# Mixture-of-experts layer on one Trainium2 core: expert outputs scaled when they leave PSUM and added to their tokens by accumulating scatters, bias and residual summed on TensorE in the last stage, one expert tile a turn

## The reference, cut to what matters

```python
x = layer_norm(DN_ALPHA * x + g1 * mix, ln1_g, ln1_b)      # kept in DRAM as x1
h = modulate(x, sh2, sc2)                                   # kept in DRAM as h2
logits = t @ w_router + b_router
top_vals, top_idx = top_k(logits, 4)
probs = softmax(top_vals)
# rows sorted by expert; for each (token, choice) of an expert:
gu = xs @ w_gu[e] + b_gu[e]
act = (min(up) + 1) * min(gate) * sigmoid(1.702 * gate)     # with clips at 7
out = act @ w_down[e] + b_down[e]
ffn[token] = sum over its 4 choices of probs * out
x = layer_norm(DN_ALPHA * x + g2 * ffn, ln2_g, ln2_b)
```

## Time and profile before

| | |
|---|---|
| time, median of 3 runs | 6377.13 us (6376.93 to 6379.13) |
| the profiled execution's own time | 6380.74 us |
| its span in the profile | 6379.1 us |
| mean granted TensorE clock | 0.96 of full speed (2.4 GHz) |
| PE, PEld, DVE, ACT, POOL busy | 93%, 75%, 71%, 49%, 15% of the span |
| `combine`, from its first instruction to the end | 6137.4 to 6379.1 us |

### The profile page before, as it was taken

How to read it: one execution, slowest core, us unless ns; L and a number is a source line. 1 busy time by engine, 2 the same in 40 slices (tenths; PEclk the granted TensorE clock), 3 DMA queues, 4 the chain that set the end, 5 groups by cost and what they waited for, 6 DMA issues and landing times. The chain is left out here.

```text
span 6379.1 us, 79201 instructions
## 1 busy us (share of the span) xinstructions
PE 5918.1 (93%) x27928; PEld 4771.0 (75%) x27928; DVE 4515.7 (71%) x3453; ACT 3133.3 (49%) x2805; POOL 980.5 (15%) x855
## 2 busy tenths in 40 slices
PE   7899999998999979998779999999999999999961
PEld 2688888886777767776668888888888888888840
DVE  3333300225656555557889999999999999999988
ACT  4222211003444434431147777777777777777730
POOL 1100000003333321114400000000000000000037
PEclk8999999999999999998889999999999999999975
DMA  5421211113444445544265542234483594214345
GB/s 215 154 79 69 79 69 69 47 45 122 135 132 140 130 164 186 173 138 159 96 247 231 221 157 97 77 151 164 176 363 125 201 414 188 103 41 180 137 151 191
DMA packets 306183, 959.46 MB, mean 150 GB/s; under 512 B 26498, under 2 KB 163970, under 8 KB 269474
## 3 DMA queue, kind: packets, MB, share of 16 engines
q1 hardware_dynamic: 204626, 684.81, 29.0%
q0 software_dynamic: 53808, 231.01, 9.9%
q10 hardware_dynamic: 47616, 41.95, 1.9%
HBM read 770.75 MB, written 186.93 MB: 150 GB/s over the span
## 5 line engine op out<-in xcount | busy, mean ns | idle before, releaser
L1901 DVE TENSOR_TENSOR moe_w_lo<-moe_w_gu,moe_w_hi 128x2048 fp32r<-128x2048 f32 x672 | 1494.1, 2285 | 3.3 <-ACT moe_w_hi L1857 3.3
L1857 ACT CAST moe_w_hi<-moe_w_gu 128x2048 fp32r<-128x2048 f32 x672 | 1287.4, 1917 | 398.7 <-PE moe_ps_gu L1803 205.4
L1907 DVE TENSOR_TENSOR moe_w_lo<-moe_w_dn,moe_w_hi 128x2048 fp32r<-128x2048 f32 x332 | 752.0, 2286 | 33.9 <-ACT moe_w_hi L1864 33.9
L1864 ACT CAST moe_w_hi<-moe_w_dn 128x2048 fp32r<-128x2048 f32 x332 | 637.5, 1920 | 264.8 <-PE moe_ps_gu L1803 264.8
L1803 PE MATMUL moe_ps_gu<-moe_w_hi,moe_hT_hi 128*128 128x512 f32 x2688 | 728.8, 393 | 12.3 <-DVE moe_w_lo L1901 12.3
L1803 PE MATMUL moe_ps_gu<-moe_w_hi,moe_hT_lo 128*128 128x512 f32 x2688 | 720.1, 390 | 0.0
L1803 PE MATMUL moe_ps_gu<-moe_w_lo,moe_hT_hi 128*128 128x512 f32 x2688 | 719.8, 390 | 0.0
L167 PE MATMUL prj_ps_p<-h_hi,prj_w_hi 128*128 128x512 f32 x1792 | 698.2, 390 | 15.6 <-DVE prj_w_lo L526 15.6
L167 PE MATMUL prj_ps_p<-h_lo,prj_w_hi 128*128 128x512 f32 x1792 | 698.0, 390 | 0.0
L167 PE MATMUL prj_ps_p<-h_hi,prj_w_lo 128*128 128x512 f32 x1792 | 697.9, 389 | 0.0
L1803 PEld LDWEIGHTS moe_ps_gu<-moe_w_lo,moe_hT_hi 128*128 128x128 f32 x2688 | 505.6, 188 | 105.7
(11 more groups left out here) (303 smaller groups left out, 9624.5 us busy)
## 6 DMA issues: line engine op xcount, KB each, us to landing
moe_w_gu<-in_w_gu_t SPq DMA_DIRECT2D x128, 2048.0 KB, 9.3
moe_w_dn<-in_w_down_t SPq DMA_DIRECT2D x64, 2048.0 KB, 8.8
rows_scratch<-prj_out POOLq DMA_DIRECT2D x48, 1024.0 KB, 4.3
brn_w<-in_w_branch_t SPq DMA_DIRECT2D x64, 768.0 KB, 6.6
slot_out_scratch<-moe_rows POOLq DMA_DIRECT2D x82, 512.0 KB, 2.9
prj_w<-in_w_in_t SPq DMA_DIRECT2D x80, 512.0 KB, 4.3
moe_b_gu<-b_gu_scratch SPq DMA_DIRECT2D x32, 1024.0 KB, 8.2
rows_scratch<-ssd_out ACTq DMA_DIRECT2D x96, 256.0 KB, 2.9
```

The lines of the kernel that those rows point to most:

```text
L1857: act.copy(w_hi[n % NB][:], raw(w_gu, n)).then_inc(gu_hi, 1)
L1864: act.copy(w_hi[(GU + n) % NB][:], raw(w_dn, n)).then_inc(dn_hi, 1)
L1901: dve.tensor_tensor(w_lo[n % NB][:], raw(w_gu, n), w_hi[n % NB][:].bitcast(F32), ALU.subtract).then_inc(gu_lo, 1)
L1907: dve.tensor_tensor(w_lo[b][:], raw(w_dn, n), w_hi[b][:].bitcast(F32), ALU.subtract).then_inc(dn_lo, 1)
```

## The change

1. `whole_tiles`: `slot_out_scratch` is gone. A new DRAM tensor `sum_scratch` (2048 + 128 rows) takes its place, and POOL fills it with zeros: one memset, then 17 stores of 512 KB in place of 32.
2. `route`: beside the token of each slot PE now also sums its probability. The moving operand of the 64 products is twice as wide (200 columns), DVE builds `pick_row` and the half scaled by the probability, POOL builds the half scaled by the token number (64 `tensor_scalar`). Behind the sums DVE derives three tables: `slot_prob`, `slot_token`, and `slot_home` (the row of `sum_scratch` that a slot is added to; unused slots go to the 128 spare rows).
3. `experts`: one step a loop turn instead of two, under an `If` on the number of tiles itself. ACT evicts with a scale per partition (`slot_prob`) in place of a copy. POOL copies the slots' row numbers and issues an indirect DMA that adds the 128 rows to `sum_scratch` in DRAM, after a wait for the one before it.
4. `combine`: no gathers. SP loads the summed tile beside x1. PE sums in PSUM: probabilities x (bias x g2) and a matmul of x1 with DN_ALPHA x identity, both in float32. DVE multiplies the sum by g2, adds PSUM, takes the statistics. ACT normalises. The product with `ln_g` goes from POOL to DVE, in the step two later. POOL only adds `ln_b`. A tile's buffers are reloaded when its product with `ln_g` is done.

```diff
 (whole_tiles, POOL)
-                with pool.Fori(SEQ * TOPK // P, MOE_TILES) as i:
-                    pool.dma_start(S.slot_out_d[bass.ds(i * P, P), :], h_hi[:, 0, 0:D].bitcast(F32)).then_inc(filled, 16)
+                pool.memset(zero[:], 0.0).then_inc(zeroed, 1)
+                pool.wait_ge(zeroed, 1)
+                for t in range(TT + 1):
+                    pool.dma_start(S.sum_d[t * P:(t + 1) * P, :], zero[:]).then_inc(filled, 16)
 (route)
+                pool.wait_ge(placed, 1)
+                for j in range(TT * TOPK):
+                    pool.tensor_scalar(pick_col[:, j, 0, :], iota_t[:], slot_col[:, j:j + 1], token[:, j // TOPK:j // TOPK + 1],
+                                       ALU.is_equal, ALU.mult).then_inc(token_picks, 1)
...
                 for j in range(TT * TOPK):
-                    pe.wait_ge(picks, j + 1)
-                    last = pe.matmul(psK[:, 0:MOE_COLS], pick_row[:, j, :], pick_col[:, j, :], start=j == 0, stop=j == TT * TOPK - 1)
+                    pe.wait_ge(row_picks, j + 1)
+                    pe.wait_ge(token_picks, j + 1)
+                    last = pe.matmul(psK[:, 0:2 * MOE_COLS], pick_row[:, j, :], pick_col[:, j, :, :].rearrange("p a c -> p (a c)"),
+                                     start=j == 0, stop=j == TT * TOPK - 1)
...
-                    dve.tensor_scalar(pick_col[:, j, :], iota_t[:], slot_col[:, j:j + 1], token[:, j // TOPK:j // TOPK + 1],
-                                      ALU.is_equal, ALU.mult).then_inc(picks, 1)
+                    dve.tensor_scalar(pick_col[:, j, 1, :], iota_t[:], slot_col[:, j:j + 1], S.probs[:, j:j + 1],
+                                      ALU.is_equal, ALU.mult).then_inc(row_picks, 1)
 (experts)
-            with eng.Fori(LEAD, MOE_ROUNDS) as r:
-                with eng.If(r < rounds_less_2 + 2):
-                    for s in range(2):
-                        step(lambda lag, fn, *more: at(r, s, lag, fn, *more))
+            with eng.Fori(LEAD, MOE_STEPS) as r:
+                with eng.If(r < count + 4):
+                    step(lambda lag, fn, *more: at(r, lag, fn, *more))
...
                     pool.wait_ge(rows_kept, i + 1)
+                    wait(pool, stored, 16 * i)
                     apart(pool, S)
-                    pool.dma_start(S.slot_out_d[bass.ds(i * P, P), :], rows[:]).then_inc(stored, 16)
+                    pool.tensor_copy(home_i[:], S.slot_home[:, bass.ds(i, 1)]).then_inc(homed, 1)
+                    pool.wait_ge(homed, i + 1)
+                    apart(pool, S)
+                    pool.indirect_dma_start(S.sum_d, bass.IndirectOffsetOnAxis(ap=home_i[:], axis=0), rows[:], None,
+                                            compute_op=ALU.add).then_inc(stored, 16)
...
                     wait(act, stored, 16 * i)
-                    act.copy(rows[:], psD[:]).then_inc(rows_kept, 1)
+                    act.activation(rows[:], psD[:], ACT.Identity, scale=S.slot_prob[:, bass.ds(i, 1)]).then_inc(rows_kept, 1)
 (combine, SP)
-                    wait(sp, stats, t - SLOT + 1)
+                    wait(sp, scaled, t - SLOT + 1)
                     apart(sp, S)
                     sp.dma_start(x1[s][:], S.x1_d[bass.ds(t * P, P), :]).then_inc(x1_in[s], 16)
+                    sp.dma_start(acc[s][:], S.sum_d[bass.ds(t * P, P), :]).then_inc(acc_in[s], 16)
 (combine, PE)
+                    wait(pe, added, t - 1)
+                    pe.wait_ge(x1_in[s], 16 * (t // SLOT + 1))
                     for c in range(D // BANK):
                         cols = slice(c * BANK, (c + 1) * BANK)
-                        last = pe.matmul(psB[t % 2][:, cols], denseT[:, t * P:(t + 1) * P], b_dn[:, cols], start=True, stop=True)
+                        pe.matmul(psB[t % 2][:, cols], denseT[:, t * P:(t + 1) * P], b_dn[:, cols], start=True, stop=False)
+                        last = pe.matmul(psB[t % 2][:, cols], alpha[:], x1[s][:, cols], start=False, stop=True)
 (combine, ACT)
+                    act.wait_ge(shifted, t + 1)
+                    act.activation(acc[s][:], acc[s][:], ACT.Identity, bias=nb[s][:], scale=rs[s][:]).then_inc(normed, 1)
 (combine, DVE: blend, invert, scale at lags 0, 1, 2)
+                    dve.wait_ge(acc_in[s], 16 * (q + 1))
+                    dve.tensor_tensor(acc[s][:], acc[s][:], g2[:], ALU.mult).then_inc(gated, 1)
+                    dve.wait_ge(gated, t + 1)
+                    dve.wait_ge(rested, t + 1)
+                    dve.tensor_tensor(acc[s][:], psB[s % 2][:], acc[s][:], ALU.add).then_inc(added, 1)
...
+                    dve.wait_ge(normed, t + 1)
+                    wait(dve, stored[s], 16 * q)
+                    dve.tensor_tensor(yo[s][:], acc[s][:], lg[:], ALU.mult).then_inc(scaled, 1)
```

More of the change, by code:

```diff
@@ L1695, in _ @@
                 chain.step(dve.tensor_copy(S.fresh[:], fresh[:]))
[L1697 to L1700 removed]
+                chain.step(dve.tensor_copy(S.tiles[:], cum[a][:, E - 1:E]))
                 dve.wait_ge(listed, 1)
[L1702 to L1703 removed]
+                chain.step(dve.tensor_copy(S.slot_prob[:], psK[:, MOE_COLS:2 * MOE_COLS]))
+                chain.step(dve.tensor_scalar(found[:], psK[:, 0:MOE_COLS], -1.0, 0.0, ALU.add, ALU.max))
+                chain.step(dve.tensor_copy(S.slot_token[:], found[:]))
+                chain.step(dve.tensor_scalar(vacant[:], psK[:, 0:MOE_COLS], 0.0, None, ALU.is_equal))
+                chain.step(dve.scalar_tensor_tensor(out=found[:], in0=vacant[:], scalar=spare[:, 0:1], in1=found[:],
+                                                    op0=ALU.mult, op1=ALU.add))
+                chain.step(dve.tensor_copy(S.slot_home[:], found[:]))
 def experts(nc, A, S, sem, sems):
@@ L1729, in experts @@
         rows = sb("rows", [P, D])
-        tok_i = pair("tok_i", [P, 1], I32)
+        tok_i = sb("tok_i", [P, 1], I32)
         psG = ps("gu", [P, F2])
@@ L1786, in step @@
                     at(0, fetch_tokens)
-                less_2 = tiles(pool, step)
-                pool.wait_ge(x_in, 32 * less_2 + 64)
+                count = tiles(pool, step)
+                pool.wait_ge(x_in, 16 * count + 64)
                 apart(pool, S)
-                pool.wait_ge(stored, 32 * less_2)
+                pool.wait_ge(stored, 16 * count)
                 apart(pool, S)
@@ L1982, in step @@
                     at(1, fetch_bias_gu)
-                less_2 = tiles(sp, step)
+                count = tiles(sp, step)
                 for landed, past in ((gu_in, 48), (dn_in, 32), ([bgu_in], 48)):
                     for part in landed:
-                        sp.wait_ge(part, 32 * less_2 + past)
+                        sp.wait_ge(part, 16 * count + past)
                         apart(sp, S)
@@ new lines, in blend @@
+                    dve.wait_ge(acc_in[s], 16 * (q + 1))
[3 more added lines that the diff above has]
+                    dve.tensor_tensor(acc[s][:], psB[s % 2][:], acc[s][:], ALU.add).then_inc(added, 1)
+                    dve.wait_ge(added, t + 1)
+                    for half in range(2):
+                        dve.bn_stats(st[s][:, half, :], acc[s][:, half * BANK:(half + 1) * BANK]).then_inc(halves, 1)
```

203 lines of the change are left out of this document (93 added, 110 removed).

## The result

The kernel with the change takes 6308.78 us (median of 4 runs, 6307.81 to 6309.32), the kernel before 6377.03 on the same chip: a ratio of 0.9893 (95% interval 0.9877 to 0.9908), 68 us less. The forecast was 6279 us, range 6245 to 6325. So sign and range are right, and 30 us of the expected gain are missing.

The account below looks back on a forecast made before the run. PE was taken to bound the expert loop, with DVE 0.4 us a step behind. -34.4 + 19 - 1 - 81.8 = -98.2 against 6380.74 gave 6282.5; a median 3.6 lower gave 6279 us, range 6245 to 6325.

Parts of the forecast that it names:

- One turn less: Expert loop: 85 steps instead of 86, saving one full step, -34.4 us; the doubled number of branches costs nothing.
- Eviction, copy, scatter, bandwidth at nothing: Expert loop: the scaled eviction, POOL's copy and scatter, its landing and its extra traffic are all hidden, 0 us.
- The rival with a late scatter: Expert loop: each us of scatter landing beyond 30 adds 1 us to 81 steps, 6441 at 32 us; chance 4%.
- the one with DVE bound by descriptors: Expert loop: descriptors written while DVE needs the port add 81 x 0.8 = +65 us, 6344; chance 7%.
- The routing stage: Routing: POOL's picks add +18 us to DVE's line (0 to +31), three more table steps 1 us.
- The fill: Zero fill at the start: 17 stores for 32, -1 us (0 to -3).
- The last stage: `combine`: 160.2 us instead of 242, saving -81.8 us (bounds -57 to -102).
- PE: four float32 products are eight passes: Last stage, PE's part of a two-tile cycle: 3.6 us at 2.4 GHz to 7.2 at 1.2 GHz, taken as 5.4.
- PE always at the low clock: Rival, last stage: PE stays at the low clock throughout, 6290 us; chance 20%.
- The outer bounds: Whole kernel: the time with all the terms' bounds on one side, 6241 or 6319 us.

Follow-up runs that it names:

- e3: The changed kernel with the table of tiles saying one tile more, so the expert loop makes one more turn: 6341.61 us, ratio 0.9953.
- e4: The changed kernel with the expert loop's end at 86 instead of 100, so one turn is skipped instead of 15: 6298.38 us, ratio 0.9886.
- e2: The changed kernel with the last stage's alpha*x1 added by VectorE instead of TensorE for all tiles: 6280.36 us, ratio 0.9857.
- e10: On top of e5, alpha*x1 is added by TensorE for even tiles and by VectorE for odd ones: 6261.86 us, ratio 0.9823.
- e5: The changed kernel with eight last-stage slots instead of four, and SyncE storing tile t-6 instead of t-3 behind the loads: 6275.50 us, ratio 0.9843.
- e9: On top of e5, 24 fp32r products ahead of the first tile and four behind each float32 pair, sums thrown away: 6243.75 us, ratio 0.9797.
- e6: The changed kernel with 24 fp32r products added on TensorE in the last stage while it waits for parameters: 6308.78 us, ratio 0.9899.
- e7: The changed kernel with every eighth token pick of the routing stage on VectorE, the other 56 on GpSimd: 6306.43 us, ratio 0.9895.
- e11: e2 (alpha*x1 added by VectorE for all tiles) with e5's eight slots and loads ahead: 6275.58 us, ratio 0.9846.

## Why the prediction was right, and where not

**One turn less: right.** -34.4 us predicted; steps of 34.44 us before and 34.43 after, and e3 gets a turn's price back. Beside the loop I took the doubled number of turns as free. In turns with work it is; the eight further skipped turns at the end cost 6 us (e3, e4), a term that the sum did not have.

**Eviction, copy, scatter, bandwidth at nothing: right.** DVE waits 27.1 us where it waited 28.0. The scatter lands after 7.5 us, where 30 were to be had. The estimate by the Trainium skill (Collectives: The Full Stack, "The bandwidth ceiling: the fold count and why AG ≠ RS ≠ AR"), twice 2.9 us, was 1.7 us short; against the same indirect transfer without the addition the ratio is 7.5 / 4.5 = 1.7. The rival with a late scatter and the one with DVE bound by descriptors are dead. POOL's part was costed far too low: it issues for 2.8 us at each scatter (223.8 us in 81), not 1, and the copy ahead of it takes 1.7 us, not 0.48. But POOL has 11.6 us to spare a step, and DVE loses nothing.

**The routing stage: size nearly right by luck, mechanism wrong.** +19 predicted, +13.6 measured. I let DVE pay for POOL's picks, at 0.285 us a pick, the price of another operation. DVE hardly pays, 2.6 us in 128 picks. POOL pays: 0.6 us a pick alone, 0.66 beside DVE, 2.7 us lost to the wide comparison, and its last pick, 16.9 us behind DVE's, sets the sums. That the earlier trace rows, where DVE waited for a POOL operation of 2.34 us, would hold as well for operations of 0.3 us was the wrong step. For operations that long it does hold, as e2 and e10 show. And the earlier trace rows do not agree with a full wait as closely as I wrote: POOL's rest of 2.31 us and DVE's own 0.81 make 3.12 us, 0.26 more than the 2.86 there, not 0.1.

**The fill: cannot be told.** First picks came 5.5 us earlier, but in the twelve experiments, whose code is the same up to there, they come at 3174.53 to 3189.49 us. The difference lies within what one kernel does from run to run. In the stretch 206 to 260 us PE is busier, 50.04 us for 43.33, but in the twelve experiments it is anything from 37.8 to 50.1 there, so that tells nothing either.

**The last stage: the failed step.** I costed it at 160 us and it takes 190, over the 185 from which on I had called myself wrong. The structure was right (the loads queue behind the store, pairs of tiles, PE in the cycle) and so was its first product's time, 11.4 us after the start for 11.3. The term that was mis-sized is "PE: four float32 products are eight passes", 3.6 to 7.2 us, of which I took the middle, 5.4. It measures 8.0 to 8.2 us: the clock is at 0.50 all the time, and a pass takes 1.0 us, not 0.86. In the earlier trace rows the products of a tile share their weights, here the weights change with each product, and 0.28 us a product come on top; that the weight loads are the cause is not shown.

By the parts of the sum: start to the first finished product 39.9 us for 31, six cycles 127.6 for 108.3, the odd tile 8.0 for 6.3, the end 14.4 for 14.6. PE's term is 2.8 us of the 3.2 that a cycle has too much, three times that at the start, where the sums of three tiles stand ahead of the first finished product, and all of the odd tile's 1.7: 26 of the 30 us. The rival "PE always at the low clock", 6290 us, had the mechanism and too small a price for it: 7.2 us, and in the six cycles only. e5 and e2 show that PE's time is what the cycle pays, e9 that the clock is: at 1.00 the same passes take half.

**The sum.** That 6309 us lies within the range owes something to luck: 30 us of the last stage and 6 of the seam are missing, and 10 us of that come back from two places that I had not costed so: 5 from the routing stage, where the mechanism was another, and 5 from first picks that came early. The outer bounds were also added up a little wrong, 6241 and 6319; the terms give 6239 and 6318.

## What to carry to other kernels

Price a float32 matmul at the clock that its own stretch will have, from rows in which the weights change as often as in the new code, and not by the middle between two clocks: when work moves to TensorE as the idle engine, it may become the bound at half speed. Where two engines hold each other up, look for rows with operations as long as the new ones, and see who waits there. A ring of buffers does not bring a load forward while the load stands behind a store in the issuing engine's program.

## What the runs showed of the hardware that I had not expected

- With TensorE busy 20.00 of 20 us on float32 products of 512 columns the granted clock was 0.50 (e5); with four fp32r products added behind each pair of them it was 1.00, and the stage with twice the passes was 32 us shorter (e9).
- Behind 24 fp32r products the granted clock was 1.00 through 3.75 us of idle time and fell to 0.50 within 2 us of float32 work (e6).
- A `tensor_scalar` of 128 x 100 with two per-partition scalars takes GpSimd 0.6 us with VectorE idle, VectorE about 0.24 a pick; taking eight of 64 from GpSimd made the other 56 no faster as a whole (e7).
- A scatter of 128 rows of 4 KB lands after 7.5 us with addition, 4.5 us without; a plain store of the same rows after 2.9.
- A skipped turn of the five-engine loop costs 0.8 us (e3; eight turns between the kernels before and after: 6.0 us).
- VectorE's operation on 1024 columns with both inputs in SBUF took 3.25 us for 1.22 beside GpSimd's addition (e2, e10, e11); the one with an input in PSUM kept its 1.22 us (e10).
- GpSimd is busy 2.8 us issuing an indirect scatter of 128 rows, 1.0 issuing a gather (kernel after).
